# A mixture-of-experts encoder block: scatter and gather moved inside the first product, the last expert written out by itself, the closing norm on two engines

## The reference, cut to what matters

```
h   = rmsnorm(x) ; proj = h @ w_in + b_in            # 1024 x 4352
oa  = neighbourhood attention(proj) ; ob = sliding-window attention(proj)
x   = x + (sigmoid(ga) * (oa @ w_up_a) + sigmoid(gb) * (ob @ w_up_b)) @ w_out
h2  = rmsnorm(x)
top-4 of 32 experts per token, softmax over the four router logits
per expert e:  gu   = h2[its tokens] @ w1[e] + b1[e]           # 1024 x 2048
               gate = min(gu[:, :1024], 7) ; up = clip(gu[:, 1024:], -7, 7)
               hid  = (up + 1) * gate * sigmoid(1.702 * gate)
               y[its tokens] += share * (hid @ w2[e] + b2[e])  # 1024 x 1024
out = rmsnorm(x + y) * final_g
```

## Time and profile before

| | us |
|---|---|
| median of 3 runs | 1141.22 |
| lowest, highest | 1140.94, 1141.25 |
| the profiled execution's own time | 1141.12 |
| its span in the trace | 1139.3 |
| TensorE busy | 1078.2 (95%) |
| VectorE busy | 285.8 (25%) |
| ScalarE busy | 102.2 (9%) |
| read from memory | 434.98 MB |

### The profile page before, as it was taken

One profiled execution on the slowest core, in us unless ns is written; L12 is line 12 of the kernel. 1 busy time (PEld: TensorE's weight loads), 2 busy tenths in 40 slices (PEclk: granted clock), 3 DMA queues, 4 the chain that ended last, 5 costly groups with the idle time before them and its releaser, 6 DMA issues.

```text
span 1139.3 us, 13050 instructions
## 1 busy us (share of the span) xinstructions
PE 1078.2 (95%) x5177; PEld 474.2 (42%) x5177; DVE 285.8 (25%) x614; ACT 102.2 (9%) x215; POOL 11.2 (1%) x20
## 2 busy tenths in 40 slices
PE   7999999899999999999999999999999999999996
PEld 6788788733333333333333333333233323333332
DVE  4652422322222222222222222221211112222222
ACT  1121430200000000000000000000000000000001
POOL 1100000000000000000000000000000000000000
PEclk9999999999999999999999999999999999999999
DMA  9963158589999999999999999999999999999994
GB/s 364 370 258 123 60 224 349 203 350 399 427 429 427 430 427 429 429 427 430 427 430 427 430 427 429 429 427 430 427 429 428 430 427 429 429 427 430 427 430 193
DMA packets 35378, 436.31 MB, mean 383 GB/s; under 512 B 5312, under 2 KB 5696, under 8 KB 7488
## 3 DMA queue, kind: packets, MB, share of 16 engines
q1 hardware_dynamic: 34640, 435.63, 91.3%
q10 hardware_dynamic: 720, 0.42, 0.1%
HBM read 434.98 MB, written 1.05 MB: 383 GB/s over the span
## 4 chain that ended last, share of the span: by engine, by line
PE 71%; DMA 18%; SPq 6%; DVE 4%; issue 1%; ACT 0%; another core or an unknown queue 0%; POOL 0%; DVEq 0%; POOLq 0%; ACTq 0%
PE bank L762 27%; DMA ring<-in_w 17%; PE bank L791 15%; PE bank L490 8%; SPq L342 5%; PE bank L729 4%; PE bank L679 4%; PE bank L685 3%; PE bank L604 2%; PE bank L586 2%; DVE work L1118 1%; PE bank L747 1%; PE bank L525 1%; PE bank L539 1%; DMA ring<-in_w_in 1%; PE bank L510 1%
## 5 line engine op out<-in xcount | busy, mean ns | idle before, releaser
L762 PE MATMUL bank<-ring,work 128*64 128x512 f32 x2048 | 451.1, 593 | 22.6 <-DMA ring<-in_w 21.8
L762 PEld LDWEIGHTS bank<-ring,work 128*64 128x64 f32 x2048 | 144.4, 137 | 309.4 <-issue 259.1
L791 PE MATMUL bank<-ring,work 128*64 128x512 f32 x1024 | 235.5, 602 | 18.1 <-DVE work L1118 18.1
L791 PEld LDWEIGHTS bank<-ring,work 128*64 128x64 f32 x1024 | 68.2, 137 | 142.0 <-issue 116.3
L1109 DVE TENSOR_SCALAR work<-bank 128x512 f32<-128x512 f32 x32 | 22.1, 692 | 418.0 <-PE bank L762 418.0
L490 PE MATMUL bank<-ring 128*128 128x256 f32 x432 | 96.5, 381 | 0.0
L1228 ACT ACTIVATE work<-work 128x512 f32<-128x512 f32 x32 | 20.1, 629 | 758.4 <-DVE work L1109 758.4
L490 PEld LDWEIGHTS bank<-ring 128*128 128x128 f32 x432 | 81.1, 190 | 13.2 <-issue 2.4
L679 PE MATMUL bank<-x2n,work 128*64 128x512 f32 x264 | 63.9, 604 | 0.8 <-DVE work L1024 0.8
L729 PE MATMUL bank<-work 64*128 64x512 f32 x256 | 63.6, 615 | 0.9 <-DVE work L1122 0.9
L1044 DVE TENSOR_TENSOR work<-bank,vec 128x256 f32<-128x256 f32 x66 | 25.0, 420 | 141.2 <-PE bank L685 141.2
(11 more groups left out here) (174 smaller groups left out, 441.6 us busy)
## 6 DMA issues: line engine op xcount, KB each, us to landing
ring<-in_w SPq DMA_DIRECT2D x192, 2048.0 KB, 40.7
ring<-in_w_in SPq DMA_DIRECT2D x16, 1024.0 KB, 17.5
ring<-in_w_out SPq DMA_DIRECT2D x4, 1024.0 KB, 4.7
ring<-in_w_up_a SPq DMA_DIRECT2D x2, 1024.0 KB, 12.2
ring<-in_w_up_b SPq DMA_DIRECT2D x2, 1024.0 KB, 7.6
ring<-in_na_rpb SPq DMA_DIRECT2D x1, 1536.0 KB, 18.4
out<-x2n SPq DMA_DIRECT2D x4, 256.0 KB, 2.1
ring<-in_consts SPq DMA_DIRECT2D x1, 864.0 KB, 13.3
```

Of the source, the lines that this page charges most:

```text
L762: last = pe.matmul(bank[CAP * a:CAP * (a + 1), bk, :], kT, pairs[:, pair_of(par, k // 2), at + q * 512:at + (q + 1) * 512], start=False, s ...
L791: last = pe.matmul(bank[CAP * a:CAP * (a + 1), BH, :], fT, pairs[:, pair_of(par, c), at + a * 512:at + (a + 1) * 512], start=f == 0, stop= ...
```

## The change

1. **TensorE's block.** `scatter()` moves from behind k = 7 to ahead of k = 4, and `gather()` to ahead of k = 6. Both stand behind the wait for the chunk of that k. Nothing then stands between k = 7 and the wait for `hid_ready`. This holds for all blocks (block 0 has no scatter).
2. **The last two experts stand behind the loop.** The loops on SyncE and TensorE end one round of two experts earlier and blocks 30 and 31 are written out; on VectorE it is block 31. The last leaves out `turn_gathered()` and `scale_gathered()`, which would serve a block that doesn't come. Its chunk 3 is loaded in two transfers of 1 MB and its chunk 5 in one of 1 MB and two of 0.5 MB, each with a semaphore of its own, and k = 6, 7 and f = 4, 6, 7 wait for these.
3. **The closing norm.** ScalarE squares each 512-column bank by itself and scales by 1/D on the way. VectorE meanwhile multiplies the banks by final_g, in the opposite order of the halves. After GpSimd's power VectorE scales the left half and ScalarE the right half; SyncE writes out the left halves and ScalarE issues the right ones.

```diff
@@ SyncE @@
-            with sp.Fori(1, E // 2) as j:
+            with sp.Fori(1, E // 2 - 1) as j:
                 for par in range(2):
                     for c in range(BLK):
                         load_chunk(2 * j + par, c, par, (2 * j + par - 2) * BLK + (PRE + c + 1))
+            for c in range(BLK):
+                load_chunk(E - 2, c, 0, (E - 4) * BLK + PRE + c + 1)
+            for c in range(BLK):
+                if c not in LAST_CUTS:
+                    load_chunk(E - 1, c, 1, (E - 3) * BLK + PRE + c + 1)
+                    continue
+                sp.wait_ge(chunk_used, (E - 3) * BLK + PRE + c + 1)
+                for n, cols in LAST_CUTS[c]:
+                    sp.dma_start(pairs[:, pair_of(1, c), cols], pair_source(E - 1, c, cols)).then_inc(piece_landed[n], 16)
...
-                for a in range(2):
-                    sp.wait_ge(out_ready, 2 * m + a + 1)
-                    sp.dma_start(out[0, m * P:(m + 1) * P, a * 512:(a + 1) * 512],
-                                 x2n[:, m, a * 512:(a + 1) * 512]).then_inc(out_stored, 16)
+                sp.wait_ge(out_ready, m + 1)
+                sp.dma_start(out[0, m * P:(m + 1) * P, 0:512], x2n[:, m, 0:512]).then_inc(out_stored, 16)
@@ TensorE, expert_block @@
                 for k in range(D // P):
-                    if k % 2 == 0:
+                    if last_one and k // 2 == 3:
+                        pe.wait_ge(piece_landed[k - 6], 16)
+                    elif k % 2 == 0:
                         pe.wait_ge(pair_landed[par][k // 2], landings)
+                    if k == 4 and not first:
+                        pe.wait_ge(down_ready, b)
+                        scatter()
+                    if k == 6:
+                        pe.wait_ge(pick_ready, b + 2)
+                        gather()
...
-                if not first:
-                    pe.wait_ge(down_ready, b)
-                    scatter()
-                pe.wait_ge(pick_ready, b + 2)
-                gather()
                 pe.wait_ge(hid_ready, b + 1)
                 turn(BH, lambda j: hid[:, j * P:(j + 1) * P], 4, hidT_done)
...
-                    if f == TURN_F:
+                    if f == TURN_F and not last_one:
                         pe.wait_ge(xg_ready, b + 2)
                         turn_gathered()
...
-            with pe.Fori(1, E // 2) as j:
+            with pe.Fori(1, E // 2 - 1) as j:
                 for par in range(2):
                     expert_block(2 * j + par, par, j * 16 + 16)
+            expert_block(E - 2, 0, E // 2 * 16)
+            expert_block(E - 1, 1, E // 2 * 16, last_one=True)
@@ VectorE, end @@
+            def weigh(m, a):
+                return dve.tensor_tensor(x2n[:, m, a * 512:(a + 1) * 512], bank[:, BY + 2 * m + a, :],
+                                         gf_b[:, a * 512:(a + 1) * 512], ALU.mult)
+            def mean_square(m):
+                dve.wait_ge(square_act, 2 * m + 2)
+                dve.tensor_scalar(msq[:, 2, m:m + 1], ssq[:, 0, m:m + 1], ssq[:, 1, m:m + 1], EPS,
+                                  ALU.add, ALU.add).then_inc(msq_ready, 1)
+            def scale_out(m):
+                dve.wait_ge(rstd_ready, 3 + m)
+                dve.wait_ge(z_done, 2 * m + 2)
+                dve.tensor_scalar(x2n[:, m, 0:512], x2n[:, m, 0:512], rstd[:, 2, m:m + 1], None,
+                                  ALU.mult).then_inc(out_ready, 1)
             for m in range(MT):
...
+                dve.wait_ge(y_done, m + 1)
+                weigh(m, 1).then_inc(z_done, 1)
+                dve.wait_ge(square_act, 2 * m + 1)
+                weigh(m, 0).then_inc(z_done, 1)
+                if m == 0:
+                    mean_square(0)
+            scale_out(0)
+            mean_square(1)
+            scale_out(1)
@@ ScalarE, end @@
             for m in range(MT):
                 act.wait_ge(y_done, m + 1)
-                act.activation(x2n[:, m, :], bank[:, BY + 2 * m:BY + 2 * m + 2, :].rearrange("p b n -> p (b n)"), ACT.Square,
-                               accum_out=ssq[:, 2, m:m + 1]).then_inc(ssq_act, 1)
+                for a in range(2):
+                    if a:
+                        act.wait_ge(z_done, 2 * m + 1)
+                    act.activation(junk[:, 2 * m + a, :], bank[:, BY + 2 * m + a, :], ACT.Square, scale=D ** -0.5,
+                                   accum_out=ssq[:, a, m:m + 1]).then_inc(square_act, 1)
+            for m in range(MT):
+                act.wait_ge(rstd_ready, 3 + m)
+                act.activation(x2n[:, m, 512:D], x2n[:, m, 512:D], ACT.Identity, scale=rstd[:, 2, m:m + 1]).then_inc(act_out, 1)
+                act.wait_ge(act_out, m + 1)
+                act.dma_start(out[0, m * P:(m + 1) * P, 512:D], x2n[:, m, 512:D]).then_inc(out_stored, 16)
```

More of the change, by code:

```diff
@@ L192, in build_block @@
         vec = sb("vec", [P, n_vec])
+        junk = pairs[:, 2, 0:2048].rearrange("p (n d) -> p n d", n=4)
         gf_b = pairs[:, 1, 0:D]
@@ L250, in build_block @@
         pool_step = sem("pool_step")
-        ones_set, ssq_act = sem("ones_set"), sem("ssq_act")
+        ones_set = sem("ones_set")
         msq_ready, rstd_ready = sem("msq_ready"), sem("rstd_ready")
@@ L269, in build_block @@
         scatT_done, scatT_ready, down_ready, scatter_done = sem("scatT_done"), sem("scatT_ready"), sem("down_ready"), sem("scatter_done")
+        piece_landed = [sem(f"last_piece_landed{n}") for n in range(5)]
+        z_done, square_act, act_out = sem("z_done"), sem("square_act"), sem("act_out")
         y_done, out_ready, out_stored = sem("y_done"), sem("out_ready"), sem("out_stored")
@@ L283, in landings @@
             return 16 * (chunk // SLOTS + 1)
+        LAST_CUTS = {3: [(0, slice(0, 2048)), (1, slice(2048, 4096))],
+                     5: [(2, slice(0, 2048)), (3, slice(2048, 3072)), (4, slice(3072, 4096))]}
         def pair_of(par, c):
@@ L342, in load_chunk, with pair_source @@
                 sp.dma_start(pairs[:, pair_of(par, c), :], pair_source(blk, c)).then_inc(pair_landed[par][c], 16)
-            def pair_source(e, c):
+            def pair_source(e, c, cols=slice(0, PAIR_F)):
                 w, at = (w1, c) if c < W1_CH else (w2, c - W1_CH)
-                return w[bass.ds(e, 1), at].rearrange("e p n -> p (e n)")
+                return w[bass.ds(e, 1), at, :, cols].rearrange("e p n -> p (e n)")
             for n in range(1, PRE):
@@ L748, in add_b1, with expert_block @@
                               start=True, stop=False)
-            def expert_block(b, par, landings, first=False):
+            def expert_block(b, par, landings, first=False, last_one=False):
                 if not first:
@@ L782, in expert_block @@
                     c = W1_CH + f // 4
-                    if f % 4 == 0:
+                    if last_one and f in (4, 6, 7):
+                        pe.wait_ge(piece_landed[2 + (4, 6, 7).index(f)], 16)
+                    elif f % 4 == 0:
                         pe.wait_ge(pair_landed[par][c], landings)
                     at = f % 4 * D
-                    if f == TURN_F:
+                    if f == TURN_F and not last_one:
                         pe.wait_ge(xg_ready, b + 2)
@@ L807, in _ @@
             expert_block(1, 1, 16)
-            with pe.Fori(1, E // 2) as j:
+            with pe.Fori(1, E // 2 - 1) as j:
                 for par in range(2):
                     expert_block(2 * j + par, par, j * 16 + 16)
+            expert_block(E - 2, 0, E // 2 * 16)
+            expert_block(E - 1, 1, E // 2 * 16, last_one=True)
             n_over = pe.value_load(ctrl[0:1, OVER:OVER + 1], min_val=0, max_val=OVER_MAX)
             with pe.If(n_over > 0):
+                pe.wait_ge(xg_ready, E + 1)
+                turn_gathered()
                 with pe.Fori(0, OVER_MAX) as j:
@@ L1093, in _, with expert_block @@
             STEPS = 2
-            def expert_block(b, first=False):
+            def expert_block(b, first=False, last_one=False):
                 one, nxt = bass.ds(b, 1), bass.ds(b + 1, 1)
@@ L1118, in expert_block @@
                 dve.tensor_copy(hidT, bank[:, BH, :]).then_inc(hidT_ready, 1)
-                scale_gathered(b + 1)
+                if not last_one:
+                    scale_gathered(b + 1)
                 dve.wait_ge(chunk_used, b * BLK + PRE + BLK)
@@ L1125, in _ @@
             expert_block(0, first=True)
-            with dve.Fori(1, E) as b:
+            with dve.Fori(1, E - 1) as b:
                 expert_block(b)
+            expert_block(E - 1, last_one=True)
             n_over = dve.value_load(ctrl[0:1, OVER:OVER + 1], min_val=0, max_val=OVER_MAX)
             with dve.If(n_over > 0):
+                scale_gathered(E)
                 with dve.Fori(0, OVER_MAX) as j:
@@ L1135, in _ @@
             dve.wait_ge(final_g_landed, 16)
-            for m in range(MT):
[L1137 to L1144, removed]
+            def weigh(m, a):
[10 more added lines that the diff above has]
```

(4 more changed lines are left out.)

## The result

The changed kernel takes 1262.61 us (median of 4 runs, 1261.12 to 1262.88) against 1141.24: ratio 1.1055, 95% interval 1.1041 to 1.1069. It is 121 us slower: the direction was forecast, and the size is 17.6 us above the 1245 of the forecast. The profiled execution took 1262.37 us, with a span of 1260.5.

The account below looks back on a forecast made before the run. TensorE was taken to bound blocks 2 to 18 and weight transfers the later ones. 1141.12 + 65.4 (wait) - 0.6 (last expert) - 0.5 (norm) = 1205.4, plus 40.3 of clock falls = 1245.7; stated 1245 us, range 1225 to 1262.

Parts of the forecast that it names:

- What bounds the kernel: Block loop: TensorE paces at 27.15 us a block through block 18, then weight transfers at 29.37 us.
- The wait behind w1: TensorE, w1's end to transposes: VectorE's chain uncovered, 2.93 us a block, making blocks 30.08 us without clock falls.
- That case: Rival in the loop: TensorE waits but its granted clock stays 1.00, total 1205 us; chance 27%.
- The clock: TensorE around w2: idle drops the clock to 1.2 GHz in most blocks, 1.3 us each, 40.3 us in all.
- Stays low for longer: Rival in the loop: clock not granted again as w2 starts, 2.4 us lost a block, 1280 us; chance 9%.
- evenly from block 1 to 31: Profile sign: VectorE's line 1109 clamps evenly 30.1 us apart, or about 31.4 with clock falls, never 29.37.
- block 0's 1.70: First 16 instructions of w2 in block 0: 1.70 us lost to a clock fall, counted in the sum.
- The last expert in pieces: Last block: transfers in pieces gain 0, since TensorE doesn't wait for the last chunks at 30 us a block.
- The closing norm: End of kernel, first square to last scaling: 0.5 us faster, between -1.5 and +1.
- The other side: Rival: weight transfers still set the pace and the pieces gain at the tail, 1137.4 us; chance 4%, 3 of it faster.

Follow-up runs that it names:

- experiments 5: Changed kernel with the gather back behind k = 7, only the scatter inside w1: 1159.75 us, ratio 1.0167.
- experiment 6: Changed kernel with the scatter back behind k = 7, only the gather inside w1: 1143.76 us, ratio 1.0017.
- the filled kernel: Changed kernel plus six unread products, alternating column halves, between w1 and the wait for hid_ready in blocks 1 to 31: 1208.39 us, ratio 1.0587.
- experiment 1: Kernel before with only the move of scatter and gather into w1: 1263.67 us, ratio 1.1066.
- experiment 9: Kernel before plus the written-out last blocks and their pieces alone, old order and old norm: 1139.04 us, ratio 0.9981.
- experiment 7: Changed kernel with scatter and gather inside w1 in block 31 alone, old order in blocks 0 to 30: 1143.54 us, ratio 1.0009.
- the kernel with no move: Changed kernel with scatter and gather back behind k = 7, everything else kept: 1138.55 us, ratio 0.9969; run again, 1138.95 us, ratio 0.9977.

## Why the prediction was right, and where its sizes were off

**What bounds the kernel** was read rightly: TensorE's 27.15 us a block with 2.2 us to spare against the weights. A wait of 2.93 goes past that mark, and experiments 5 and 6 show that one of about 1.0 sets the blocks at 28.36 and 28.01, and that without the falls little is lost: experiment 6 is 2.5 us above the kernel before.

**The wait behind w1** (2.93 us) is exact: the filled kernel's clamps are 30.08 apart, the number of the forecast. That case was put at 1205, and 1208.4 was measured. In its profiled execution (1209.61) the first clamp comes at 251.58, not at 248.32, and block 0 lost 2.55 to the clock instead of the 1.70 of the sum; both come from falls of the clock outside the filled blocks (near 56 and 226 us, and in block 0).

**The clock** is the term that was mis-sized. The prediction took 1.3 us a block, between bounds of 0 and 1.70. Measured are 2.68, 1.44 and 1.22 in turn (the intervals less 30.08), 1.78 in the mean, and every third block is above the upper bound, because there the low stretch is twice as long (6.8 against 3.4 us). The mean lies inside the prediction's own 0.65 to 1.85, near its upper end, and so the 1262.6 lies at the very edge of its 1225 to 1262. "Stays low for longer" had been put aside as a rival for all blocks, when it holds for every third. The sign "evenly from block 1 to 31" failed with it. The one fall in the kernel before could not show this, and it was itself chance: the prediction put block 0's 1.70 into its sum as fixed, and in the seven other traces in which block 0's gather stands behind w1 the clock did not fall there. The mean should have been formed over where the fall lands, ahead of the transposes, at them or behind them. What was missed is 31 x 0.48 = 15 of the 17 us between 1245.7 and the 1262.4 of the profiled execution. Another 1.25 came before the blocks began, and is chance too (experiment 1's trace has no such fall, its first clamp is at 248.64): the first clamp is at 249.57 instead of 246.45 + 1.87 = 248.32, and the windows of the changed kernel show a low clock where the kernel before had none:

```profile
52.00:55.00 3.00, 0.97 (x5) 0.80 0.96 404
55.00:58.00 3.00, 3.00 (x15) 0.63 1.02 426
```

The rule of the Trainium skill ("TensorE: Matmul & The Clock Gate", the section on HAM oscillation), a wait in each round of a loop throttles the clock in each round, agrees with the trace of the changed kernel: 31 of 31 here. It does not hold for every wait: experiment 6 has one of 0.94 us in each of 31 blocks, and the clock fell in none. Its half of the throttled time, an estimate worked out for low stretches of 3.4 and 6.8 us as in these windows, would be 1.7 and 3.4; measured 1.2 to 1.4 and 2.7, since a part of each low stretch lies on idle.

**The last expert in pieces**: worth nothing under the move, as said; 2.2 us without it (experiment 9). **The closing norm**: -0.5 forecast, -0.76 in the profile (the last scaling on ScalarE took 0.72, not 0.60, and the steps before it less than put down).

**The other side**, transfers that still pace, did not happen. Its price of 1137.4 was also wrong by its own steps. It let k = 7 follow the last piece with scatter and gather done in waiting time; experiment 7 shows that there is no such waiting time once chunk 3 comes in pieces. What gives 1138 is the pieces with the old order.

## What to carry to other kernels

Work that stands between a product and its consumer on the same engine may be a cover, not an obstacle: before it is moved, take the length of the chain on the other engines that runs beside it, and compare what stays uncovered with the engine's slack per round (here 2.93 against 2.22). An idle stretch of TensorE in every round can have a second price, the clock, which here was four fifths of the first; filling it with useless products gives that part back, but the other part only goes if real work is put there. And price a periodic fall of the clock over all positions in the round, not from one instance.

## What the runs showed of the hardware that was not expected

Twelve float32 instructions of 512 columns into the same 64 columns of the array take 5.25 us; alternating between the two halves they take 2.75 at most, 0.23 each, at the same granted clock of 1.00. The same block in the same program took 31.29, 31.52 or 32.76 us in a strict order of three, with the place where the clock fell. And part of the 2 to 4 us by which executions of one kernel differ is the clock: of the kernel with no move there are two traces. In the one that took 1137.31 us it fell nowhere before the end; in the one that took 1140.53 it fell near 55 and 222 us, and its first clamp came 3.3 us later (250.19 against 246.90).
